# Order changed at four seams of a two-block kernel, and the FFN's up projection with a 512-column operand

## The reference

```python
def hgrn2_chunk_scan(q, k, v, b):       # gated linear attention, per head
    ...                                  # scores from q, k and decays; o = scores @ v + q @ state
def _modulate(h, shift, scale):
    return h * (1 + scale) + shift
def _conv_ffn(h, w_up, conv_w, conv_b, w_down):
    gate, up = jnp.split(h @ w_up, 2, axis=-1)      # w_up: 1024 x 5632
    gate = _dwconv(gate, conv_w, conv_b)            # 3 taps along the tokens
    return (jax.nn.silu(gate) * up) @ w_down        # w_down: 2816 x 1024
# end of the second block:
#   att = softmax(q k^T * scale + bias) v over 8 heads;  x = x + mod[2] * mix_out(att, ...)
#   h2 = _modulate(_rmsnorm(x, norm2_g), mod[3], mod[4])
#   x  = x + mod[5] * _conv_ffn(h2, ...);  return _rmsnorm(x, final_norm_g)
```

## Time and profile before

| | us |
|---|---|
| median of 3 runs | 848.49 (848.02 to 849.5) |
| the profiled execution | 849.81 |
| its span (first to last instruction) | 848.6 |
| TensorE busy | 819.3 |
| VectorE busy | 592.6 |
| ScalarE busy | 460.5 |
| mean granted clock of TensorE | 0.993 |

### The profile page before, as it was taken

One profiled execution on the slowest core, in us unless ns is written; L12 is line 12 of the kernel. 1 busy time (PEld: TensorE's weight loads), 2 busy tenths in 40 slices (PEclk: granted clock), 3 DMA queues, 4 the chain that ended last, 5 costly groups with the idle time before them and its releaser, 6 DMA issues.

```text
span 848.6 us, 13159 instructions
## 1 busy us (share of the span) xinstructions
PE 819.3 (97%) x5363; PEld 714.4 (84%) x5363; DVE 592.6 (70%) x843; ACT 460.5 (54%) x764; POOL 48.1 (6%) x67
## 2 busy tenths in 40 slices
PE   9999999999998998998999999997998999999996
PEld 7998988878997997997988789884466999999995
DVE  6765455646799798798785886897928765666564
ACT  6645444445577857857756552555635544444432
POOL 8100002600000000000000000000000000000000
PEclk9999999999999999999999999999998999999998
DMA  8879875783643443445346763845536455556531
GB/s 286 300 256 242 242 248 199 234 297 118 196 142 107 150 149 108 141 149 188 111 157 234 272 236 131 317 150 194 183 143 222 150 198 192 168 187 199 187 111 49
DMA packets 102631, 160.07 MB, mean 189 GB/s; under 512 B 11318, under 2 KB 67994, under 8 KB 100267
## 3 DMA queue, kind: packets, MB, share of 16 engines
q1 hardware_dynamic: 102570, 159.24, 57.1%
HBM read 156.02 MB, written 3.21 MB: 188 GB/s over the span
## 4 chain that ended last, share of the span: by engine, by line
PE 85%; DVE 7%; ACT 4%; DMA 3%; issue 2%; POOL 0%; POOLq 0%; DVEq 0%
PE acc L448 12%; PE acc L450 12%; PE acc L449 12%; PE acc L477 9%; PE acc L479 9%; PE acc L478 9%; PE misc L1185 2%; PE misc L2169 2%; PE misc L2167 2%; PE misc L2168 2%; PE misc L864 1%; PE misc L587 1%; DMA raw<-in_w_in_dram 1%; DVE soft L1984 1%; PE misc L1290 1%
## 5 line engine op out<-in xcount | busy, mean ns | idle before, releaser
L421 DVE TENSOR_TENSOR w_lo<-raw,w_hi 128x2048 fp32r<-128x2048 f32 x114 | 263.4, 2320 | 105.6 <-ACT w_hi L414 105.6
L414 ACT ACTIVATE w_hi<-raw 128x2048 fp32r<-128x2048 f32 x114 | 217.4, 1911 | 109.3 <-PE acc L450 26.6
L448 PE MATMUL acc<-XH,w_hi 128*128 128x256 f32 x848 | 242.8, 286 | 0.0
L449 PE MATMUL acc<-XL,w_hi 128*128 128x256 f32 x848 | 240.9, 284 | 0.0
L450 PE MATMUL acc<-XH,w_lo 128*128 128x256 f32 x848 | 240.8, 284 | 0.0
L448 PEld LDWEIGHTS acc<-XH,w_hi 128*128 128x128 f32 x848 | 163.1, 192 | 4.2 <-issue 1.8
L449 PEld LDWEIGHTS acc<-XL,w_hi 128*128 128x128 f32 x848 | 163.2, 192 | 0.8
L450 PEld LDWEIGHTS acc<-XH,w_lo 128*128 128x128 f32 x848 | 163.0, 192 | 0.0
L477 PE MATMUL acc<-w_hi,XH 128*128 128x512 f32 (+1 forms) x224 | 87.4, 390 | 0.8 <-DVE w_lo L421 0.8
L479 PE MATMUL acc<-w_hi,XL 128*128 128x512 f32 (+1 forms) x224 | 85.6, 382 | 0.0
L478 PE MATMUL acc<-w_lo,XH 128*128 128x512 f32 (+1 forms) x224 | 85.6, 382 | 0.0
(11 more groups left out here) (280 smaller groups left out, 1333.5 us busy)
## 6 DMA issues: line engine op xcount, KB each, us to landing
raw<-in_hgrn_w_in_dram SPq DMA_DIRECT2D x32, 1024.0 KB, 5.7
ada_raw<-in_ada_w_dram SPq DMA_DIRECT2D x24, 1024.0 KB, 7.2
raw<-in_ffn_w_up_dram SPq DMA_DIRECT2D x22, 1024.0 KB, 5.1
...
```

The source lines that it names most:

```text
L414: self.hi_done.up(act.activation(self.w_hi[v % RING][:, 0:w], self.raw[j][:, 0:w], ACT.Copy), v)
L421: self.lo_done.up(dve.tensor_tensor(self.w_lo[j][:, 0:w], self.raw[j][:, 0:w], self.w_hi[v % RING][:, 0:w].bitcast(F32), ALU.subtract), v)
L448: pe.matmul(o, wh[:, k, c:c + P], xh[:, k, :], start=k == 0, stop=False)
L449: pe.matmul(o, wh[:, k, c:c + P], xl[:, k, :], start=False, stop=False)
```

## The change

1. Scores: in `act_hgrn` the even pairs' first score copies move ahead of the forget tiles' sigmoids, and the odd pairs' head scalings move between the two query copies.
2. Exponentials: the first head's exponentials (and a weight unit's high part) move into `act_in2`, ahead of the last query tile's copy. Two exponential buffers get a place of their own for that. Of four weight units whose low and high parts were made within the attention loops, one low part goes ahead and two behind it. Ada piece 12 moves to the stage's begin.
3. Modulation: ada pieces 20 and 21 (`2 * KD + 4`, `+ 5`) move from before the last output part to behind it, beside 22 and 23.
4. Last norm: the gain is multiplied in per chunk, half 0's root moves ahead of half 1's chunks, and the scaling by the reciprocal root is one instruction on VectorE and one on ScalarE per half.
5. Up projection: `XH` and `XL` become the two halves of one tensor `X2`. `project_wide` multiplies the high weights with both in one matmul of 512 columns, into a whole bank, and the low weights with `XH` into the bank's first half: two matmuls per step. The bank's halves are added by a ScalarE copy of one half and a VectorE addition of the other.

```diff
@@ -124,8 +124,9 @@
         x_at = self.top
-        self.XH = new("XH", [KD, TOK], F32R)
-        self.XL = new("XL", [KD, TOK], F32R)
+        self.X2 = new("X2", [2, KD, TOK], F32R)
+        self.XH, self.XL = self.X2[:, 0], self.X2[:, 1]
         self.ident = new("ident", [P])
@@ -448,6 +451,29 @@
             m = pe.matmul(o, wl[:, k, c:c + P], xh[:, k, :], start=False, stop=k == K - 1)
+        assert self.tile_done.up(m) == t
+        self.over(self.tile_done, v)
+    def project_wide(self, u, n, col, ready=None):
+        pe, (t, b, use) = self.nc.tensor, self.tiles_of[u][n]
+        v = next(v for v in self.slab[u] if self.unit[v].c0 <= col < self.unit[v].c0 + self.unit[v].n)
+        (wh, wl), c = self.weights(v), col - self.unit[v].c0
+        self.unit_ready(v)
+        if use:
+            pe.wait_ge(self.acc_free[b].h, use)
+        o, low = self.acc[b][:, :].rearrange("p (a t) -> p a t", a=2), self.acc[b][:, 0:TOK]
+        for k in range(KD):
+            if ready:
+                ready(k)
+            both = self.X2[:, :, k, :]
+            if k < KD - 1:
+                pe.matmul(o, wh[:, k, c:c + P], both, start=k == 0, stop=False)
+                pe.matmul(low, wl[:, k, c:c + P], self.XH[:, k, :], start=False, stop=False)
+            else:
+                pe.matmul(low, wl[:, k, c:c + P], self.XH[:, k, :], start=False, stop=False)
+                m = pe.matmul(o, wh[:, k, c:c + P], both, start=False, stop=True)
         assert self.tile_done.up(m) == t
@@ -1382,14 +1408,15 @@
             for h in range(2):
+                if h and q is not None:
+                    self.act_scale_of(q)
                 b = self.complete(act, query, h)
                 self.freed(query, h, act.activation(self.queries_of(QK, h), acc[b][:, 0:TOK].rearrange("p (a t) -> p a t", a=2),
                                                     ACT.Copy))
-            if q is not None:
-                self.act_scale_of(q)
             self.hi(self.first(query) + RING)
             if q is not None:
                 self.act_heads_high(q, 0)
+            if p > 1:
                 self.act_scores_of(p - 1, 0)
@@ -1407,8 +1434,8 @@
                                     scale=l1), "factors", p, h)
-                if p and q is None and h == 0:
-                    self.act_scores_of(p - 1, 0)
+                if p == 1 and h == 0:
+                    self.act_scores_of(0, 0)
             self.hi(self.first(forget) + RING)
@@ -1788,6 +1815,8 @@
                 A.up(act.activation(self.MIXH[:, 4:6, :], self.U[:, :, :], ACT.Copy), "mix_gate")
+                self.hi(self.first(q, 0) + RING)
+                self.act_exp(0)
     def conv_taps(self, k0, k1):
@@ -1869,7 +1898,8 @@
         V.up(dve.tensor_tensor(uv, uv, mv, ALU.mult), "gated2")
-        self.lo(self.first(v, 0) + RING)
+        for n in range(2):
+            self.lo(self.first(v, n) + RING)
     def dve_mix(self, name, k, src):
@@ -1922,6 +1952,7 @@
         pe = self.nc.tensor
+        self.pe_ada(12)
         for n in range(4):
@@ -1962,14 +1993,12 @@
     def act_attention(self):
-        for s in range(self.STEPS):
+        for s in range(1, self.STEPS):
             self.act_exp(s)
-            if s:
-                self.act_turned(s - 1)
+            self.act_turned(s - 1)
             if s > 2 and s % 2:
                 self.act_finish(s // 2 - 1)
-            if s in (2, 4):
-                self.hi(self.first(self.u_q, s // 2 - 1) + RING)
+        self.hi(self.first(self.u_q, 1) + RING)
         self.act_turned(self.STEPS - 1)
@@ -2002,20 +2031,21 @@
         self.dve_softmax(0)
-        for s in range(self.STEPS):
+        self.dve_normalize(0)
+        self.dve_softmax(1)
+        self.dve_mix("mix_conv", 6, self.CA)
+        self.dve_mix("mix_gate", 4, self.U)
+        for s in range(1, self.STEPS):
             if s + 1 < self.STEPS:
                 self.dve_softmax(s + 1)
             if s == 3:
                 self.dve_ada(1)
             self.dve_normalize(s)
-            if s == 0:
-                self.dve_mix("mix_conv", 6, self.CA)
-                self.dve_mix("mix_gate", 4, self.U)
             if s > 2 and s % 2:
                 self.dve_finish(s // 2 - 1)
-            if s in (1, 4, 6):
-                self.lo(v + (1, 4, 6).index(s) + 1)
         self.dve_ada(2)
+        for n in range(2, 4):
+            self.lo(v + n)
         self.dve_finish(3)
@@ -2068,14 +2098,12 @@
         self.pe_out2_part(1, 0, (4, 5, 6, 7, 0, 1, 2, 3))
-        self.pe_ada(2 * KD + 4)
-        self.pe_ada(2 * KD + 5)
         self.pe_out2_part(1, 1, (4, 5, 6, 7))
         for c in range(2):
             self.pe_turn("ffn", 0, c, self.XN3)
         self.pe_out2_part(1, 1, (0, 1, 2, 3))
-        self.pe_ada(2 * KD + 6)
-        self.pe_ada(2 * KD + 7)
+        for a in range(2 * KD + 4, 3 * KD):
+            self.pe_ada(a)
         for c in range(2):
@@ -2149,8 +2177,7 @@
         for n in range(4):
-            self.project(self.u_up[i], n, n * P, (self.XH, self.XL), KD,
-                         self.both_ready("ffn") if i == 0 and n == 0 else None)
+            self.project_wide(self.u_up[i], n, n * P, self.both_ready("ffn") if i == 0 and n == 0 else None)
     def pe_down(self, i):
@@ -2190,7 +2217,7 @@
                     act.wait_ge(self.V.h, self.V["ffn_tap", i - 2, 2, f])
-                self.freed(u, f, act.activation(GP[:, f, 1:1 + TOK], acc[b][:, 0:TOK], ACT.Copy))
+                A.up(act.activation(GP[:, f, 1:1 + TOK], acc[b][:, 0:TOK], ACT.Copy), "gp", i, f)
             self.hi(self.first(u, 0) + RING)
@@ -2201,7 +2228,11 @@
             for f in range(2):
-                self.wait_freed(act, u, 2 + f)
+                b = self.complete(act, u, 2 + f)
+                if i > 1:
+                    act.wait_ge(self.V.h, self.V["ffn_rest", i - 2, f])
+                A.up(act.activation(self.UU[i % 2][:, f, :], acc[b][:, TOK:2 * TOK], ACT.Copy), "rest", i, f)
+            act.wait_ge(self.V.h, self.V["ffn_rest", i, 1])
             if i > 1:
@@ -2219,6 +2250,9 @@
                     if tap == 0:
+                        dve.wait_ge(self.A.h, self.A["gp", i, f])
+                        gp = GP[:, f, 1:1 + TOK]
+                        self.freed(u, f, dve.tensor_tensor(gp, gp, acc[self.tiles_of[u][f][1]][:, TOK:2 * TOK], ALU.add))
                         self.wait_freed(dve, u, f)
@@ -2229,9 +2263,12 @@
             for f in range(2):
+                dve.wait_ge(self.A.h, self.A["rest", i, f])
+                uu = self.UU[i % 2][:, f, :]
+                self.freed(u, 2 + f, dve.tensor_tensor(uu, uu, acc[self.tiles_of[u][2 + f][1]][:, 0:TOK], ALU.add))
+                self.wait_freed(dve, u, 2 + f)
                 dve.wait_ge(self.A.h, self.A["ffn_silu", i, f])
-                b = self.complete(dve, u, 2 + f)
-                self.freed(u, 2 + f, dve.tensor_tensor(GC[:, f, :], GC[:, f, :], acc[b][:, 0:TOK], ALU.mult))
+                V.up(dve.tensor_tensor(GC[:, f, :], GC[:, f, :], uu, ALU.mult), "ffn_rest", i, f)
             self.lo(self.first(u, 1) + RING)
@@ -2249,30 +2286,36 @@
             self.act_root("end", half, 2)
+            act.wait_ge(self.V.h, self.V["rstd", "end", half])
+            y = self.Y[:, half, 512:D]
+            self.A.up(act.activation(y, y, ACT.Copy, scale=self.nstat[:, half, 4:5]), "scaled", "end", half)
     def dve_end(self):
         dve, V = self.nc.vector, self.V
         dve.wait_ge(self.gain_in["end"].h, self.gain_in["end"]["all"])
         for half in range(2):
             for c in range(2):
                 f = slice(c * 512, c * 512 + 512)
+                x, y = self.x_tok[:, half, f], self.Y[:, half, f]
                 dve.wait_ge(self.T.h, self.T["down", half, c])
-                t = V.up(dve.tensor_tensor(self.Y[:, half, f], self.misc[2 * half + c][:, :], self.e_row[:, f], ALU.mult))
+                t = V.up(dve.tensor_tensor(y, self.misc[2 * half + c][:, :], self.e_row[:, f], ALU.mult))
                 dve.wait_ge(V.h, t)
-                V.up(dve.tensor_tensor(self.x_tok[:, half, f], self.Y[:, half, f], self.x_tok[:, half, f], ALU.add),
-                     "last", half, c)
+                t = V.up(dve.tensor_tensor(x, y, x, ALU.add), "last", half, c)
+                dve.wait_ge(V.h, t)
+                V.up(dve.tensor_tensor(y, x, self.last_row[:, f], ALU.mult))
             self.dve_part("end", half)
-        for half in range(2):
             self.dve_root("end", half)
-            self.dve_scale("end", half, self.x_tok, self.x_tok, self.last_row)
+            y = self.Y[:, half, 0:512]
+            V.up(dve.tensor_scalar(y, y, self.nstat[:, half, 4:5], None, ALU.mult), "scaled", "end", half)
     def sp_end(self):
         sp = self.nc.sync
         for half in range(2):
             for c in range(2):
-                f = slice(c * 512, c * 512 + 512)
-                sp.wait_ge(self.V.h, self.V["scaled", "end", half, c])
```

(4 more changed lines are left out.)

6 lines of the change are left out of this document (4 added, 2 removed).

## The result

| | median, us | lowest to highest | span of the profiled execution, us | its granted clock |
|---|---|---|---|---|
| before | 848.94 | 848.02 to 849.50 (4) | 848.6 | 0.993 |
| after | 836.35 | 835.84 to 837.95 (4) | 834.6 | 0.995 |

The changed kernel takes 0.9847 of the time before, 95% interval 0.9821 to 0.9872. Its profiled execution took 835.84 us, 0.5 us under its median. Forecast were 833.0 us, with a range of 829.5 to 838.5. So the sign is right and the time lies in the range, but not in the likeliest case's own range of 831.5 to 834.5: it is 3.3 us over the forecast and 1.8 us over that range.

What follows compares the result with a forecast made beforehand. TensorE, busy 819.3 of 848.6 us, bounds the kernel; -7.8 - 3.5 - 2.3 - 3.9 + 2.0 = -15.5 us takes the median from 848.49 to 833.0 us, range 829.5 to 838.5.

Steps and rivals of the forecast that it cites:

- likeliest case: Whole kernel: the forecast sum itself, 833.0 us, with 831.5 to 834.5 as its own range; chance 0.55.
- Scores, -7.8: HGRN pairs: TensorE's waits for score copies shrink by 6.1 us and those for scaled heads by 1.7, together 7.8 us.
- 6.7 + 1.7: HGRN pairs: upper bound of the gain, 8.4 us, all waits for score copies and scaled heads gone.
- Exponentials, -3.5: Attention: with the new order TensorE comes to the output projection at 610.9 instead of 614.41, 3.5 us sooner.
- from head 3 on TensorE has hardly a hole: Attention loop: from head 3, TensorE's own transposes, ada pieces and value products are the longer chain.
- Modulation, the chain, 0: Seam into the FFN: the chain from weight load to last transposes keeps its length, so 0 us gained.
- Modulation, the clock, -2.3: First FFN up projection: a hole cut from 2.7 to 1.5 us avoids the fall to 1.2 GHz, saving 2.3 us.
- The 2.25 us holes in the HGRN pairs were followed by no fall. So I take the fall as avoided: Seam into the FFN: inference that the clock stays up behind a 1.5 us hole, worth 2.3 us.
- the clock falls all the same: Rival at the seam into the FFN: the clock still falls despite the shorter hole, 835.3 us; chance 0.2.
- Up projection, -3.9: FFN up projections: one matmul start of 11 ns saved in each of 352 steps, 3.9 us; additions and copies hidden.
- Last norm, +2.0: Kernel's end: a third VectorE pass per chunk, the gain product, makes the tail 2.0 us longer.
- the bound of 2.6: Kernel's end: upper bound of the last norm's cost, +2.6 us, where both stores of the half queue.

Runs made afterwards that it cites:

- only_scores: The kernel before with the scores' order alone (score copies and head scalings moved on ScalarE): 839.85 us, 0.9897 of before.
- hi_late: The changed kernel with ScalarE's high part of the FFN's first loaded weights put behind the high parts of the FFN's input: 834.18 us, 0.9828 of before.
- only_mod: The kernel before with the modulation's order alone (ada pieces 20 and 21 behind the last output part): 847.33 us, 0.9977 of before.
- only_attn: The kernel before with the attention's order alone (the exponentials part): 845.97 us, 0.9964 of before.

## Why the prediction came out as it did

- **Scores, -7.8: right, a little small.** 8.4 us, at the bound that I had named as "6.7 + 1.7". The waits fell by 6.0 + 1.7 - 0.3 = 7.4 us, and a removed hole gave more than its length. In pair 5, from one set of scores to the next (L1178, L1204), it is 9.71 us before and 8.88 after, 0.83 less for a hole of 0.56. Part of the rest shows right behind the hole, where eight transposes take 1.16 us and otherwise 1.06; the remainder isn't explained. only_scores bears out the size.
- **Exponentials, -3.5: right.** 3.7 us, with two of five holes left. My "from head 3 on TensorE has hardly a hole" held but for one of 0.90 us.
- **Modulation, the chain, 0: right.** 13.2 us from issue to transposes for 13.0. The reason given, that Y hangs on the load through ScalarE and VectorE, is shown by hi_late: the exchange on ScalarE took 1.04 us out, which moving TensorE's pieces had not.
- **Modulation, the clock, -2.3: the step that failed.** The prediction said: "The 2.25 us holes in the HGRN pairs were followed by no fall. So I take the fall as avoided". The clock fell behind 1.77 + 0.73 us. Of the 0.94 us by which the first up projection became shorter, 0.26 are the wide operand's; the clock gave 0.7. Even these may be luck of the trace: only_scores shows the shorter low stretch with the old order and its hole, and over all runs the kernels that keep the 1.8 us hole have a mean clock of 0.9929 (18 runs) against 0.9927 for the kernel before (41). Why only_mod's twelve runs have more (0.9950) stays open. It failed as an inference from one trace: only_mod shows the clock fall behind one of those 2.24 us HGRN holes, and only_attn behind a 1.99 us one in the attention, so a hole of that size is followed by a fall in one execution and not in the next. At this seam the clock fell in all six traces with the new order and a hole of 1.6 to 1.9 us, and in none of the four in which it was filled or cut to 0.73 us. The rival "the clock falls all the same" (0.2) named it, with 835.3 us, and only its price was too high: part of the 2.3 came.
- **Up projection, -3.9: right mechanism, size off.** 11 turns at 0.26 us are 2.8 us. A merged start saves 8 ns and not 11; taking the cost of a start from 256 columns (0.120 us) and from 512 (0.229) separately and subtracting them is a difference of small differences. Neither additions nor copies showed on TensorE.
- **Last norm, +2.0: right sign, size off.** 2.7 us. The sign came from four more products in VectorE's queue, as the prediction had it. The scalings end 832.10 - 821.22 = 10.9 us after the first sum; I had 10.6. The rest is the last transfer, 2.5 us instead of 2.1, where two stores are issued together; I had left it as it was and named both stores only in the bound of 2.6.

By the rows the terms are -8.4 - 3.7 + 0.1 - 0.7 - 2.8 + 2.7 = -12.8 us, against -15.5. The 2.7 us between them are the clock (1.6), the up projection (1.1), the norm (0.7) and the chain (0.1), less 0.8 that the first two seams gave beyond the forecast. The other 0.6 us of the 3.3 are the medians': before had 848.94 us where I had started from 848.49, and the medians lie 12.6 us apart where the traces have 12.8.
